# Banded attention with outputs by token, and products of masks in the openings of the stages

## The chip, the cores and the metric

One core of one Trainium2 chip runs the whole program in one launch. The metric is device time in microseconds. The kernel before took 4315.04 us (median of 3 runs, 4312.23 to 4320.44). TensorE multiplies matrices (PE in the profile, its weight loads PEld), VectorE is DVE, ScalarE is ACT, GpSimd is POOL, SyncE is SP and issues most transfers. TensorE's clock has two levels, 1.2 and 2.4 GHz; the profile shows the granted share, 0.50 or 1.00.

## The reference

Two blocks of a transformer run one after the other on 1024 latent tokens of width 1024, the first also on 256 context tokens. The first block has two hybrid layers. Each norms and modulates the tokens, projects them, and mixes them in three ways: latent attention (6 heads), banded attention (6 query heads on 2 key heads) and a short convolution; then come an output product and 16 experts of which each takes its best tokens. The second block has gated linear attention, differential attention and a large feed-forward part. The change's larger half is in the banded attention:

```python
s_loc = jnp.einsum('bqgrd,bkgd->bgrqk', q_b, k_b).astype(jnp.float32) * SWA_SCALE
s_loc = jnp.where(valid, s_loc, -jnp.inf)           # |query - key| <= 128
s_ctx = jnp.einsum('bqgrd,bcgd->bgrqc', q_b, k_ctx).astype(jnp.float32) * SWA_SCALE
p = sink_softmax(jnp.concatenate([s_ctx, s_loc], axis=-1), sink).astype(v.dtype)
return (jnp.einsum('bgrqc,bcgd->bqgrd', p[..., :n_ctx], v_ctx)
        + jnp.einsum('bgrqk,bkgd->bqgrd', p[..., n_ctx:], v_b))
```

A block of 128 queries sees the 256 context tokens and the local keys of its own, the previous and the next block. `sink_softmax` adds one learned score per head, the sink, which takes part in the sum and has no value. In the first layer the context tokens also attend to themselves, with the same sink.

## The kernel before

The program is a series of stages. A stage is one block of the five engines' instruction streams (`k.stage()`), with a barrier between two of them, so no work of one stage runs beside another's. Inside a stage the engines are ordered by semaphores alone, each stream in the order in which it is written. Most products are made in three parts: both operands are split into a high part that ScalarE rounds and a low part that VectorE or GpSimd subtracts, and TensorE adds high x high, high x low and low x high. In the opening of such a stage TensorE therefore waits for the first split tiles.

Stages of a hybrid layer, in order, with the function and the line of the first TensorE instruction: `project_in` (1618), `window_attention` (983), `latent_projections` (1176), `latent_attention` (1297), `mixed` through `residual` and `split_linear` (792), `route` (1909), `experts` (2283), `combine` (2463). The second block runs `project2` (through `scaled_linear`, 675), `linear_attention`, `differential_attention` (2987), `residual` again (792), `feed_up` (`scaled_linear`, 675), `feed_down` (3491) and `embed_and_finish` (3320).

`window_attention` works in units: a unit is one block of 128 queries and one head. Layer 0 has 2 context blocks and 8 latent ones, 60 units; layer 1 has 48. A unit has 2 key tiles of 128 (context block), 4 (first and last latent block) or 5. For unit u:

- TensorE, `scores(u)` (lines 983 to 986): queries against keys in two passes each, and a product of a mask for a tile that is partly hidden. Scores of two units fit in PSUM, so `scores(u)` waits for the exponentials of u-2.
- VectorE, `maxima(u)` (1099, 1100): maximum of each row, and the bias for the exponentials.
- ScalarE, `exps(u)` (1054): the exponentials; then at 1058 the exponential of the sink for this unit, as a 128 x 128 tile.
- TensorE, `turned(u)` (995): one transpose for each key tile. ScalarE copies the first four back (1071), VectorE the fifth (1126).
- TensorE, `products(u)`: the sink's tile times the identity (1005), then for each tile the values (64 columns, and 64 columns of ones) as stationary operand against the turned probabilities as moving one (1012). The output has features on partitions 0 to 63 and the sums on 64 to 127, by query in columns.
- VectorE, `outputs(u)`: reciprocal of the 64 x 128 sums (1107), and the product into the mixed tensor (1109).

TensorE's loop is `turned(u)`, `scores(u+2)`, `products(u)`. ScalarE's is the copy of u, then `exps(u+1)`. VectorE's is the fifth tile of u, `maxima(u+2)`, `outputs(u-1)`. Once a block, after its third head, ScalarE and VectorE split the queries of the block after next (1046, 1092). At the start VectorE builds the sinks' tile (1113, 1115) before the first maximum.

Of the kernel before, what the change touches and what calls it, by code (L numbers as in the profile page):

```python
# [13 lines left out]
ALU = mybir.AluOpType  # L14
# [3 lines left out]
P = 128  # L18
# [48 lines left out]
class Kernel:  # L67
# [59 lines left out]
    def part(self, off, *shape):  # L127

        return self.at(off, *shape, dt=F32R)

# [510 lines left out]
def scaled_linear(k, M, w_tile, scaled, wring, whi, evict, act_work=None, dve_work=None, sync_work=None, pe_work=None):  # L641
# [4 lines left out]
    with k.stage() as (block, sem):  # L646
# [16 lines left out]
        def _(pe):  # L663
            for n in range(M):
# [79 lines left out]
def split_linear(k, M, KT, chunks, w_tile, x, evac, engines, wring, make=None, before=None, beside=None, whi=None, wide=P):  # L744
# [9 lines left out]
    with k.stage() as (block, sem):  # L754
# [22 lines left out]
        def _(pe):  # L777
            if m:
                m.begin(pe)
# [142 lines left out]
def window_attention(k, l, with_ctx):  # L922
# [9 lines left out]
    NB, H = NLAT // P, 6  # L932
    o = XT0
# [4 lines left out]
    sinks, es = k.at(o, H, P), k.at(o + H * P, 2, P)  # L938
    o += (H + 2) * P
    pr = k.at(o, 2, 5 * P)  # L940
    o += 10 * P
    pt, rec = k.at(TAB0 + 1280, 2, 5, P), k.at(TAB0 + 1280 + 10 * P, 2, P)
    mx, nb = k.at(o, 64), k.at(o + 64, 64)
    assert o + 128 <= HT0
# [7 lines left out]
    half = lambda g: slice(64 * g, 64 * g + 64)  # L952

    with k.stage() as (block, sem):
        k_hi, k_lo, q_hi, q_lo, s_full, nb_set, p_set, sk_set, own = [sem() for _ in range(9)]
        t_full, pt_a, pt_b, pv_done, r_set, o_out, blank = [sem() for _ in range(7)]
# [4 lines left out]
        def _(pe):  # L961
            def scores(u):
# [70 lines left out]
        def _(act):  # L1033
# [14 lines left out]
            def exps(u):  # L1048
                h = units[u][2]
# [16 lines left out]
            for u in range(N):  # L1066
                act.wait_ge(t_full, count_t(u) + 1)
# [4 lines left out]
                if u + 1 < N:  # L1072
                    exps(u + 1)
                if u % H == 2 and 2 <= u // H + 1 < len(blocks):
                    queries(u // H + 1)

        @block.vector
        def _(dve):
# [23 lines left out]
            def outputs(u):  # L1102
                kind, b, h = units[u]
                t0 = tokens(kind, b)
                out = k.bank[6 + u % 2]
                dve.wait_ge(pv_done, u + 1)
                dve.reciprocal(rec[0:64, u % 2, :], out[64:P, 0:P]).then_inc(r_set, 1)
                dve.wait_ge(r_set, u + 1)
                dve.tensor_tensor(MIX[half(h % 2), 3 + h // 2, t0:t0 + P], out[0:64, 0:P], rec[0:64, u % 2, :], ALU.mult).then_inc(o_out, 1)
# [11 lines left out]
            for u in range(N):  # L1121
# [11 lines left out]
            outputs(N - 1)  # L1133
# [6 lines left out]
def latent_projections(k, l, with_ctx):  # L1140
# [14 lines left out]
    with k.stage() as (block, sem):  # L1155
# [11 lines left out]
        def _(pe):  # L1167
            for x, (kind, m, t0, n) in enumerate(items):
# [67 lines left out]
def latent_attention(k, l, with_ctx):  # L1236
# [47 lines left out]
    with k.stage() as (block, sem):  # L1284
# [4 lines left out]
        def _(pe):  # L1289
            def rough(p):  # L1290
# [212 lines left out]
def project_in(k, l, with_ctx):  # L1503
# [37 lines left out]
    with k.stage() as (block, sem):  # L1541
# [26 lines left out]
        def _(pe):  # L1568
            def sums(n):
# [281 lines left out]
def route(k, l, with_ctx):  # L1851
# [26 lines left out]
    with k.stage() as (block, sem):  # L1878
# [25 lines left out]
        def _(pe):  # L1904
            def raw(c):
# [238 lines left out]
def experts(k, l, with_ctx):  # L2144
# [37 lines left out]
    with k.stage() as (block, sem):  # L2182
# [85 lines left out]
        def _(pe):  # L2268
            def transposes(e, i, j, steady):
# [165 lines left out]
def combine(k, l, with_ctx):  # L2435
# [7 lines left out]
    with k.stage() as (block, sem):  # L2443
# [10 lines left out]
        def _(pe):  # L2454
            for i in range(len(tiles)):
# [478 lines left out]
def differential_attention(k):  # L2934
# [30 lines left out]
    with k.stage() as (block, sem):  # L2965
# [8 lines left out]
        def _(pe):  # L2974
# [716 lines left out]
```

## Time and profile before

| | |
|---|---|
| median of 3 runs | 4315.04 us |
| profiled execution | 4315.07 us, span 4313.3 us |
| TensorE busy | 3876.7 us, 90% |
| TensorE weight loads | 3083.9 us, 71% |
| VectorE, ScalarE, GpSimd busy | 2183.9, 1300.4 and 511.2 us (51%, 30%, 12%) |
| granted clock over the span | 0.946 |
| banded attention, first to last product | 301.8 to 466.8 us and 1741.3 to 1879.2 us |

The span begins with the program's first instruction on the core. TensorE's records overlap, since products are pipelined; the distance between two starts is what a product costs in a series, not its length. A wait is put down to whoever ended it. The clock share of a window is a mean: a window of 0.50 was wholly at the low level.

### The profile page before, as it was taken

How to read it: one execution, taken by the hardware profiler on the slowest of the kernel's cores; microseconds unless marked ns; L12 is line 12 of the kernel's file. 1: busy time of each engine (PE TensorE's matmuls, PEld its weight loads, DVE VectorE, ACT ScalarE, POOL GpSimd, SP SyncE). 2: the span in 40 equal slices, each digit the busy share in tenths (PEclk: the TensorE clock that was granted, in tenths of full speed). 3: DMA queues.
4: the chain of work that ended last, by engine and by line, in shares of the span. 5: the costliest groups of instructions: out<-in, count | busy, mean ns of one | idle time of the engine just before them, and what ended most of it. 6: DMA issues, size and time to landing. Idle time of an engine off the chain costs nothing. (4 is left out here: it accounts for less than half of the span.)

```text
span 4313.3 us, 51341 instructions
## 1 busy us (share of the span) xinstructions
PE 3876.7 (90%) x20508; PEld 3083.9 (71%) x20508; DVE 2183.9 (51%) x3383; ACT 1300.4 (30%) x2259; POOL 511.2 (12%) x601
## 2 busy tenths in 40 slices
PE   7989899887999889889985998799777899998997
PEld 5879665665777679866664998587555688887875
DVE  3479666333222256876534333583664465553344
ACT  3226533231111042553313333312453211112241
POOL 1010211103222110021012111100102100000011
PEclk9999899998999999989997999899888999999998
DMA  6100000448777431000025996212001211112111
GB/s 253 35 20 1 17 1 0 176 161 352 274 275 272 158 137 40 1 17 1 1 90 222 341 341 226 73 49 88 3 1 69 73 49 47 46 49 81 49 57 59
DMA packets 73877, 453.29 MB, mean 105 GB/s; under 512 B 8000, under 2 KB 12624, under 8 KB 57680
## 3 DMA queue, kind: packets, MB, share of 16 engines
q1 hardware_dynamic: 56960, 389.73, 24.0%
q0 software_dynamic: 13088, 47.19, 4.0%
q10 hardware_dynamic: 3632, 13.63, 0.8%
q8 instruction: 137, 2.24, 0.2%
q14 instruction: 60, 0.49, 0.0%
HBM read 394.95 MB, written 55.57 MB: 104 GB/s over the span
## 5 line engine op out<-in xcount | busy, mean ns | idle before, releaser
L2307 PEld LDWEIGHTS psum<-words,words 128*128 128x128 f32 x4096 | 513.9, 192 | 10.5 <-issue 9.2
L2307 PE MATMUL psum<-words,words 128*128 128x160 f32 (+1 forms) x4096 | 515.2, 288 | 1.5 <-DVE words L392 1.5
L675 PE MATMUL psum<-words,words 128*128 128x512 f32 x1104 | 442.3, 401 | 31.0 <-DVE words L715 26.6
L677 PE MATMUL psum<-words,words 128*128 128x512 f32 x1104 | 438.0, 397 | 0.0
L676 PE MATMUL psum<-words,words 128*128 128x512 f32 x1104 | 437.9, 397 | 0.0
L1618 PE MATMUL psum<-words,words 128*128 128x428 f32 (+1 forms) x720 | 253.3, 352 | 31.7 <-DVE words L1711 31.7
L675 PEld LDWEIGHTS psum<-words,words 128*128 128x128 f32 x1104 | 209.3, 190 | 83.7 <-DVE words L715 28.1
L1327 PE MATMUL psum<-words 128*128 128x512 f32 (+1 forms) x504 | 252.3, 582 | 0.0
L1619 PE MATMUL psum<-words,words 128*128 128x428 f32 (+1 forms) x720 | 250.0, 347 | 0.0
L1620 PE MATMUL psum<-words,words 128*128 128x428 f32 (+1 forms) x720 | 249.4, 346 | 0.0
L694 ACT ACTIVATE words<-words 128x1024 fp32r<-128x1024 f32 x69 | 73.1, 1060 | 582.3 <-DMA words<-in_w_up 382.0
L677 PEld LDWEIGHTS psum<-words,words 128*128 128x128 f32 x1104 | 209.2, 189 | 51.1
L676 PEld LDWEIGHTS psum<-words,words 128*128 128x128 f32 x1104 | 208.8, 189 | 51.0 <-issue 1.0
L1371 ACT ACTIVATE words<-psum 128x512 f32<-128x512 f32 (+1 forms) x252 | 147.7, 586 | 283.3 <-PE psum L1319 283.3
L1397 DVE TENSOR_REDUCE words<-psum 128x1 f32<-128x512 f32 (+1 forms) x300 | 163.3, 587 | 120.3 <-PE psum L1297 119.5
L792 PE MATMUL psum<-words,words 128*128 128x512 f32 (+1 forms) x448 | 173.8, 388 | 33.3 <-DVE words L515 33.1
L1317 PE MATMUL psum<-words,words 97*128 97x512 f32 (+1 forms) x252 | 195.3, 775 | 9.2 <-ACT words L1358 9.2
L591 POOL TENSOR_TENSOR words<-words 128x512 f32<-128x512 f32 (+1 forms) x56 | 76.2, 1393 | 1020.7 <-ACT words L584 1020.7
L2404 DVE TENSOR_TENSOR words<-words,psum 128x160 f32<-128x160 f32 x64 | 20.6, 322 | 316.3 <-ACT words L2367 316.3
L794 PE MATMUL psum<-words,words 128*128 128x512 f32 (+1 forms) x448 | 172.1, 384 | 0.0
L793 PE MATMUL psum<-words,words 128*128 128x512 f32 (+1 forms) x448 | 171.5, 383 | 0.0
L1618 PEld LDWEIGHTS psum<-words,words 128*128 128x128 f32 x720 | 138.1, 192 | 37.0 <-DVE words L1711 32.1
(438 smaller groups left out, 7853.2 us busy)
## 6 DMA issues: line engine op xcount, KB each, us to landing
words<-in_w_gate SPq DMA_DIRECT2D x32, 2048.0 KB, 8.2
words<-in_w_up SPq DMA_DIRECT2D x32, 2048.0 KB, 12.7
words<-in_w_down SPq DMA_DIRECT2D x32, 2048.0 KB, 13.1
words<-in_ada_w SPq DMA_DIRECT2D x24, 2048.0 KB, 14.7
words<-in_w_in SPq DMA_DIRECT2D x55, 512.0 KB, 3.4
words<-in_w_up SPq DMA_DIRECT2D x44, 512.0 KB, 3.4
words<-in_w_down SPq DMA_DIRECT2D x44, 256.0 KB, 2.6
words<-in_x SPq DMA_DIRECT2D x2, 5120.0 KB, 22.0
```

The source lines that it names most:

```text
L675: pe.matmul(out, hi[:, j, w], S.parts[0](kt, t0, nt), start=(kt == 0), stop=False)
L676: pe.matmul(out, hi[:, j, w], S.parts[1](kt, t0, nt), start=False, stop=False)
L677: mm = pe.matmul(out, lo[:, j, w], S.parts[0](kt, t0, nt), start=False, stop=(kt == KD - 1))
L792: pe.matmul(out, hi[:, j, w], x[0](kt, t0, n), start=(kt == 0), stop=False)
L793: pe.matmul(out, hi[:, j, w], x[1](kt, t0, n), start=False, stop=False)
L794: mm = pe.matmul(out, lo[:, j, w], x[0](kt, t0, n), start=False, stop=(kt == KT - 1))
L1317: pe.matmul(to, k_hi[0:ROW + 1, h % 2, key], q_hi[0:ROW + 1, h % 2, t0:t0 + n], start=True, stop=False)
L1327: pe.matmul(k.bank[O_BANK[u % 2]][:, 0:n], V[:, 6 * t + h, :], pt[:, x % R, 0:n], start=(t == 0), stop=(t == keys - 1)).then_inc(d_done, 1)
L1618: pe.matmul(out, whi[:, j, w], xhi[:, kt, c0:c0 + nc], start=(kt == 0), stop=False)
L1619: pe.matmul(out, whi[:, j, w], xlo[:, kt, c0:c0 + nc], start=False, stop=False)
L1620: mm = pe.matmul(out, wlo[:, j, w], xhi[:, kt, c0:c0 + nc], start=False, stop=(kt == KD - 1))
L2307: mm = pe.matmul(k.bank[m % 2][:, u * W:(u + 1) * W], ring[:, side[j], w0:w0 + P], xgT[:, j, kt, 0:W], start=(kt == 0), stop=(kt == KD - 1))
```

## The change

Two things are changed.

First, `keep_busy` is called at the head of TensorE's stream in twelve functions, 22 stages in all. It makes n products of 128 x 128 by 128 x 384, both operands from the constant masks (bf16), into PSUM bank 7. Nobody reads them, and they wait for nothing but the barrier. The numbers are 16 (`scaled_linear`), 20 (`split_linear`), 9 or 23 (`window_attention` of layers 0 and 1), 7 (`latent_projections`), 5 (`latent_attention`), 22 (`project_in`), 6 (`route`), 70 or 16 (`experts` of layers 0 and 1), 9 (`combine`), 5 (`differential_attention`), 16 (`embed_and_finish`), 16 (`feed_down`).

Second, in `window_attention` the value product changes sides: the turned probabilities are stationary and the values moving, 64 features and one column of ones. The output is by token: queries on partitions, and the six heads of a block side by side in one PSUM bank, 72 columns apart. The sink's tile and its product are gone. Once a block VectorE subtracts the sinks from the six biases (`arguments`), ScalarE takes six exponentials a row (`sinks`), VectorE adds them to the six sums, takes six reciprocals and norms all heads in one product (`outputs`); TensorE turns the result back with three transposes (`back`), and VectorE copies it into the mixed tensor (`place`). ScalarE's order in a unit is changed too.

```diff
+    def keep_busy(self, pe, n, bank=7):
+        for _ in range(n):
+            pe.matmul(self.bank[bank][:, 0:3 * P], self.bmask[:, 2 * P:3 * P], self.bmask[:, 0:3 * P],
+                      start=True, stop=True, skip_group_check=True)
...
             def products(u):
                 kind, b, h = units[u]
-                if u >= 2:
-                    pe.wait_ge(o_out, u - 1)
-                pe.wait_ge(sk_set, u + 1)
-                out = k.bank[6 + u % 2][:, 0:P]
-                pe.matmul(out, es[:, u % 2, :], k.ident[:, :], start=True, stop=False)
+                n = u // H
+                if h == 0 and n >= 2:
+                    pe.wait_ge(placed, n - 1)
...
-                    mm = pe.matmul(out, SV[:, 2 * tile + h % 2, :], pt[:, u % 2, t, :], start=False, stop=(t == tiles(u) - 1))
+                    mm = pe.matmul(k.bank[6 + n % 2][:, h * WIDE:h * WIDE + 65], pt[:, u % 2, t, :], SV[:, 2 * tile + h % 2, 0:65],
+                                   start=(t == 0), stop=(t == tiles(u) - 1), skip_group_check=True)
...
+            def back(n):
+                pe.wait_ge(o_out, n + 1)
+                for f in range(3):
+                    mm = pe.transpose(k.bank[6 + n % 2][:, f * P:(f + 1) * P], flat(heads[:, n % 2, 2 * f:2 * f + 2, :]), k.ident[:, :])
+                mm.then_inc(backed, 1)
...
                 products(u)
+                if u > H and u % H == 2:
+                    back(u // H - 1)
+            back(N // H - 1)
...
-                if u >= 2:
-                    act.wait_ge(pv_done, u - 1)
-                act.activation(es[:, u % 2, :], sinks[:, h, :], ACT.Exp, bias=nb[:, u:u + 1]).then_inc(sk_set, 1)
+            def sinks(n):
+                act.wait_ge(args_set, n + 1)
+                act.activation(es[:, n % 2, 0:H], es[:, n % 2, 0:H], ACT.Exp).then_inc(sk_set, 1)
...
             for u in range(N):
+                if u + 1 < N:
+                    exps(u + 1)
                 act.wait_ge(t_full, count_t(u) + 1)
...
                 act.activation(pt[:, u % 2, 0:n, :], k.bank[4][:, 0:n * P].rearrange("p (a b) -> p a b", b=P), ACT.Copy).then_inc(pt_a, 1)
-                if u + 1 < N:
-                    exps(u + 1)
                 if u % H == 2 and 2 <= u // H + 1 < len(blocks):
                     queries(u // H + 1)
+                if u % H == H - 1:
+                    sinks(u // H)
...
+            def arguments(n):
+                dve.wait_ge(nb_set, H * (n + 1))
+                dve.tensor_tensor(es[:, n % 2, 0:H], nb[:, H * n:H * (n + 1)], sink, ALU.subtract).then_inc(args_set, 1)
+
+            def outputs(n):
+                e = es[:, n % 2, 0:H]
+                per_head = e.rearrange("p (h a) -> p h a", a=1)
+                dve.wait_ge(sk_set, n + 1)
+                dve.wait_ge(pv_done, H * (n + 1))
+                if n >= 2:
+                    dve.wait_ge(backed, n - 1)
+                link(dve.tensor_tensor(per_head, sums(n)[:, :, 64:65], per_head, ALU.add))
+                link(dve.reciprocal(e, e))
+                dve.tensor_tensor(heads[:, n % 2], sums(n)[:, :, 0:64], per_head.to_broadcast([P, H, 64]), ALU.mult).then_inc(o_out, 1)
+
+            def place(n):
+                t0 = tokens(*blocks[n])
+                dve.wait_ge(backed, n + 1)
+                dve.tensor_copy(MIX[:, 3:6, t0:t0 + P], k.bank[6 + n % 2][:, 0:3 * P].rearrange("p (f c) -> p f c", c=P)).then_inc(placed, 1)
...
-            link(dve.memset(sinks[:, :, 0:64], -1e30))
-            for h in range(H):
-                link(dve.tensor_scalar(sinks[:, h, 64:P], k.ones[:, 0:64], sink[:, h:h + 1], -1.0, ALU.mult, ALU.mult))
...
                 if u + 2 < N:
                     maxima(u + 2)
-                if u:
-                    outputs(u - 1)
+                    if (u + 2) % H == H - 1:
+                        arguments((u + 2) // H)
+                if u > H:
+                    if u % H == 1:
+                        outputs(u // H - 1)
+                    if u % H == 4:
+                        place(u // H - 1)
```

## Rows read from the trace of the kernel before

**Rows 1.** Windows: stretch, length, busy us of PE, PEld, DVE, ACT, POOL, clock, DMA.
```profile
347.00:447.00 100.00, 97.94 (x869) 95.68 (x868) 91.32 (x184) 60.92 (x117) 0.00 (x0) 1.00 0.01 1
```

**Rows 2.** Timeline of TensorE's weight loads: start, length, engine, line, operation, tiles, shapes, count.
```profile
403.49 0.58 PEld L995 LDWEIGHTS psum<-ident,words 128*128 128x128 f32 x5
404.03 0.19 PEld L983 LDWEIGHTS psum<-words,words 128*128 128x128 f32 x1
404.92 0.31 PEld L1005 LDWEIGHTS psum<-ident,words 128*128 128x128 f32 x2
405.15 1.20 PEld L1012 LDWEIGHTS psum<-words 128*128 128x128 f32 x10
406.27 0.58 PEld L995 LDWEIGHTS psum<-ident,words 128*128 128x128 f32 x5
```

**Rows 3.** Windows, sum line of the eight dense openings at the low clock.
```profile
sum 40.57, PE 39.04 PEld 33.71 DVE 25.76 ACT 27.02 POOL 0.00; mean PE 4.88 PEld 4.21 DVE 3.22 ACT 3.38 POOL 0.00
```

**Rows 4.** Windows, sum line of the three openings of the split product.
```profile
sum 15.62, PE 15.61 PEld 13.12 DVE 15.62 ACT 15.62 POOL 15.62; mean PE 5.20 PEld 4.38 DVE 5.21 ACT 5.21 POOL 5.21
```

**Rows 5.** Windows, sum line of the five short openings.
```profile
sum 21.33, PE 21.32 PEld 10.31 DVE 9.02 ACT 11.21 POOL 1.96; mean PE 4.26 PEld 2.06 DVE 1.80 ACT 2.24 POOL 0.39
```

**Rows 6.** Groups by line: records | busy us, mean ns | idle before.
```profile
L1012 PE MATMUL psum<-words 128*128 128x128 f32 x960 | 126.7, 277 | 0.9 <-ACT words L1071 0.9
```

**Rows 7.** Timeline of TensorE in the first stage, eight records of 2 columns.
```profile
34.40 1.05 PE L279 MATMUL psum<-add,words 128*128 128x2 f32 x8
```

**Rows 8.** Timeline of TensorE, last mask of that unit's scores.
```profile
404.92 0.23 PE L986 MATMUL psum<-bmask 128*128 128x128 bf16 x1
```

**Rows 9.** Timeline of VectorE in the same unit.
```profile
405.19 0.82 DVE L1099 TENSOR_REDUCE words<-psum 128x1 f32<-128x640 f32 x1
406.05 0.21 DVE L1100 TENSOR_SCALAR words<-words,negsink 128x1 f32<-128x1 f32 x1
406.29 0.96 DVE L1107 RECIPROCAL words<-psum 64x128 f32<-64x128 f32 x1
407.29 0.28 DVE L1109 TENSOR_TENSOR words<-psum,words 64x128 f32<-64x128 f32 x1
```

**Rows 10.** Timeline of ScalarE in the same unit.
```profile
404.23 0.60 ACT L1071 ACTIVATE words<-psum 128x512 f32<-128x512 f32 x1 [1.21 <-PE psum L995]
404.73 0.79 ACT L1054 ACTIVATE words<-psum,words 128x640 f32<-128x640 f32 x1
```

**Rows 11.** Groups by line and shape, a copy of 384 columns from PSUM.
```profile
L392 DVE COPY words<-psum 128x384 f32<-128x384 f32 x10 | 5.6, 558 | 5.6 <-PE psum L1181 5.5
```

**Rows 12.** Timeline of VectorE in a context unit.
```profile
315.60 0.42 DVE L1099 TENSOR_REDUCE words<-psum 128x1 f32<-128x256 f32 x1
```

**Rows 13.** Timeline of ScalarE in a context unit.
```profile
314.92 0.38 ACT L1071 ACTIVATE words<-psum 128x256 f32<-128x256 f32 x1 [1.22 <-PE psum L995]
315.20 0.47 ACT L1054 ACTIVATE words<-psum,words 128x256 f32<-128x256 f32 x1
```

**Rows 14.** Timeline of VectorE, opening of banded attention in layer 1.
```profile
1741.79 1.71 DVE L1115 TENSOR_SCALAR words<-ones,negsink 128x64 f32<-128x64 f32 x6
```

**Rows 15.** Timeline of TensorE, first stage of layer 0, clock rising.
```profile
61.54 0.56 PE L1619 MATMUL psum<-words,words 128*128 128x428 f32 x1
61.90 0.56 PE L1620 MATMUL psum<-words,words 128*128 128x428 f32 x1
...
62.95 0.35 PE L1618 MATMUL psum<-words,words 128*128 128x428 f32 x1
63.15 0.35 PE L1619 MATMUL psum<-words,words 128*128 128x428 f32 x1
```

**Rows 16.** Timeline of VectorE, opening of the split product after differential attention.
```profile
3290.30 13.65 DVE L515 TENSOR_TENSOR words<-words,words 128x512 fp32r<-128x512 f32 x8
```

**Rows 17.** Timeline of VectorE, opening of latent attention in layer 0.
```profile
518.58 6.35 DVE L1397 TENSOR_REDUCE words<-psum 128x1 f32<-128x512 f32 x12
```

**Rows 18.** Timeline of TensorE while the experts' results are combined in layer 0.
```profile
1500.69 1.09 PE L2463 MATMUL psum<-ident,words 128*128 128x128 f32 x8 [0.25 <-DMA words<-moe]
```

More of the change, by code:

```diff
@@ L663, in _ @@
         def _(pe):
+            k.keep_busy(pe, 16)
             for n in range(M):
@@ L777, in _ @@
         def _(pe):
+            k.keep_busy(pe, 20)
             if m:
@@ L931, in window_attention @@
     prev, nxt, idb = (k.bmask[:, n * P:(n + 1) * P] for n in range(3))
-    NB, H = NLAT // P, 6
+    NB, H, WIDE = NLAT // P, 6, 72
     o = XT0
@@ L937, in window_attention @@
     o += 12 * P
-    sinks, es = k.at(o, H, P), k.at(o + H * P, 2, P)
-    o += (H + 2) * P
+    heads = k.at(o, 2, H, 64)
+    o += 6 * P
     pr = k.at(o, 2, 5 * P)
     o += 10 * P
-    pt, rec = k.at(TAB0 + 1280, 2, 5, P), k.at(TAB0 + 1280 + 10 * P, 2, P)
-    mx, nb = k.at(o, 64), k.at(o + 64, 64)
-    assert o + 128 <= HT0
+    pt = k.at(TAB0 + 1280, 2, 5, P)
+    mx, nb, es = k.at(o, 64), k.at(o + 64, 64), k.at(o + 128, 2, 8)
+    assert o + 144 <= HT0
     blocks = ([(0, c) for c in range(CT)] if with_ctx else []) + [(1, b) for b in range(NB)]
@@ L952, in window_attention @@
     half = lambda g: slice(64 * g, 64 * g + 64)
+    sums = lambda n: k.bank[6 + n % 2][:, 0:H * WIDE].rearrange("p (h c) -> p h c", c=WIDE)
     with k.stage() as (block, sem):
         k_hi, k_lo, q_hi, q_lo, s_full, nb_set, p_set, sk_set, own = [sem() for _ in range(9)]
-        t_full, pt_a, pt_b, pv_done, r_set, o_out, blank = [sem() for _ in range(7)]
+        t_full, pt_a, pt_b, pv_done, args_set, o_out, blank, backed, placed = [sem() for _ in range(9)]
         pieces = ([(0, NCTX), (NCTX, NLAT)] if with_ctx else [(0, NT)])
@@ L961, in _ @@
         def _(pe):
+            k.keep_busy(pe, 9 if with_ctx else 23)
             def scores(u):
@@ L1048, in exps @@
             def exps(u):
-                h = units[u][2]
                 act.wait_ge(nb_set, u + 1)
@@ L1100, in maxima @@
                 dve.tensor_scalar(nb[:, u:u + 1], mx[:, u:u + 1], -SWA_SCALE, sink[:, h:h + 1], ALU.mult, ALU.min).then_inc(nb_set, 1)
[L1102 to L1109, printed above, removed]
+            def arguments(n):
[15 more added lines that the diff above has]
+                dve.tensor_copy(MIX[:, 3:6, t0:t0 + P], k.bank[6 + n % 2][:, 0:3 * P].rearrange("p (f c) -> p f c", c=P)).then_inc(placed, 1)
             queries(0)
             keys_of(0)
-            link(dve.memset(sinks[:, :, 0:64], -1e30))
-            for h in range(H):
-                link(dve.tensor_scalar(sinks[:, h, 64:P], k.ones[:, 0:64], sink[:, h:h + 1], -1.0, ALU.mult, ALU.mult))
             maxima(0)
@@ L1128, in _ @@
                     maxima(u + 2)
-                if u:
-                    outputs(u - 1)
+                    if (u + 2) % H == H - 1:
[5 more added lines that the diff above has]
+                        place(u // H - 1)
                 if u % H == 2 and 2 <= u // H + 1 < len(blocks):
                     queries(u // H + 1)
-            outputs(N - 1)
+            outputs(N // H - 1)
+            place(N // H - 1)
 KT0, V0 = PR0 + 6 * NT, PR0 + 12 * NT
@@ L1167, in _ @@
         def _(pe):
+            k.keep_busy(pe, 7)
             for x, (kind, m, t0, n) in enumerate(items):
@@ L1289, in _ @@
         def _(pe):
+            k.keep_busy(pe, 5)
             def rough(p):
@@ L1568, in _ @@
         def _(pe):
+            k.keep_busy(pe, 22)
             def sums(n):
@@ L1904, in _ @@
         def _(pe):
+            k.keep_busy(pe, 6)
             def raw(c):
@@ L2268, in _ @@
         def _(pe):
+            k.keep_busy(pe, 70 if with_ctx else 16)
             def transposes(e, i, j, steady):
@@ L2454, in _ @@
         def _(pe):
+            k.keep_busy(pe, 9)
             for i in range(len(tiles)):
@@ L2974, in _ @@
         def _(pe):
+            k.keep_busy(pe, 5)
             def scores(n):
@@ L3297, in _ @@
         def _(pe):
+            k.keep_busy(pe, 16)
             def shares(n):
@@ L3480, in _ @@
         def _(pe):
+            k.keep_busy(pe, 16)
             for s in range(S):
```

## The prediction

> **What bounds the kernel now.** The kernel is a series of 25 stages with a barrier between two of them, so what one stage loses or gains passes to the end unchanged; the span is read stage by stage. I read the windows first. Inside banded attention of the first layer TensorE is busy for 97.94 of 100 us at clock 1.00, VectorE for 91.32 and ScalarE for 60.92 [rows 1]. One (block, head) unit there with five key tiles has 25 TensorE records (5 transposes, 6 score products, 2 masks, 2 of the sink product at line 1005, 10 of line 1012), so 869 records are 34.8 units, 2.87 us each. The timeline of weight loads shows the inside of one [rows 2]: transposes 403.49 to 404.03 (0.54), scores to 404.92 (0.89), sink product to 405.15 (0.23), value products to 406.27 (1.12), sum 2.78, with no hole; the other 0.09 of the mean is where the next queries are split. So TensorE's count of passes sets the pace, and VectorE is close behind. Then I read the openings of the stages: TensorE has been idle, and its first work runs at clock 0.50 although it is busy. In the eight dense openings (both projections, both expert stages, `project2`, feed up, feed down, embed) that is 40.57 us [rows 3], in the three of the split product at lines 792 to 794 15.62 [rows 4], in five short ones 21.33 [rows 5]. These are the two places that the change touches. The profiled execution took 4315.07 us (span 4313.3), the median is 4315.04: I subtract from 4315.
>
> **Banded attention, TensorE.** Removed for each of 108 units: the sink product, 0.23. The value products keep their number: two records a tile, 960 for 480 tiles [rows 6]. They change sides: probabilities become the stationary operand (still 128 columns), values the moving one, 65 columns instead of 128. No row has 65 columns. Bounds: eight records with 2 moving columns take 1.05 us, with the length of one record (0.23, rows 8) off (1.05 - 0.23)/7 = 0.117 a pass [rows 7, 8], and with 128 columns a pass takes 1.12/10 = 0.112 [rows 2]. The ends agree to 0.005, so the stationary load sets the pass, and I take 0.112: no change.
> The Trainium skill, "TensorE: Matmul & The Clock Gate", LDWEIGHTS, puts a load at its columns over 1.2 GHz, 107 ns for 128, whatever moves; by it the value products stay as they are, and the rows agree. The same page, Back-to-back issue gap, has a product cost its moving columns over 2.4 GHz plus 2.5 ns; by that one they would get cheaper (first rival).
> Added: three transposes for a block of six units, 3 x 0.112 = 0.34, or 0.06 a unit. Its wait is for the normed outputs, which VectorE starts a whole unit earlier; behind it stand only the next unit's transposes. TensorE's own work is then 2.78 - 0.23 = 2.55.
>
> **The chain through the four engines.** ScalarE now does the exponentials of unit u+1 before it copies the turned tiles of unit u. From the start T of a unit's transposes: the scores of the unit after next end at T+0.54+0.89+0.23 (the last mask's own length, [rows 8]) = 1.66, the maximum starts at 1.70, takes 0.82 with 0.04 behind it, the bias 0.21 [rows 9]: 2.77. The exponentials follow; ScalarE's next instruction starts some 0.68 later (0.79 less an overlap of 0.1, as 404.23 to 404.73 is for a copy of 0.60), and the copy takes 0.60 [rows 10]: 4.08. That copy belongs to the next unit, whose value products TensorE could begin at P + 1.43, P the period. So P = 2.55 + (4.08 - 1.43 - P), which gives P = 2.60. The order of ScalarE costs 0.05. If the copy hides wholly, P is 2.55; if latencies are 0.17 worse twice over, it is 2.78. I take 2.60, as all terms but the order are measured. With the transposes 2.66 a unit, against 2.87: 0.21 x 72 units = 15 us. The 0.09 at the queries goes, because VectorE loses the reciprocal of 0.96 and the product of 0.28 in each unit [rows 9] and gets per block an addition, a reciprocal of six columns (each no more than about the 0.21 of a bias), a product and a copy of 384 columns from PSUM, 0.56 each [rows 11]: 1.24 a unit becomes 1.6/6 = 0.27. ScalarE loses one activation a unit.
> Context units (12, two tiles): VectorE sets them, 0.42 + 0.21 + 0.96 + 0.28 and gaps, 2.0. After, TensorE has (2+2+4) x 0.112 = 0.9 and the same chain runs 0.45 + 0.3 + 0.42 + 0.04 + 0.21 + 0.03 + 0.36 + 0.38 = 2.2 [rows 12, 13], so P = (2.2 + 0.45)/2 = 1.33; with 0.06, 0.6 saved each, 7 us; the first run at the low clock, so 6. Units of four tiles (24) stand between: 0.2 each, 5 us.
> Opening: in the second layer the first maximum waits behind the six operations at line 1115, 1.71 us [rows 14], which go; in the first layer ScalarE is later anyway. I take 1.3. End: after the last product there were 0.96 + 0.28; now three small operations, 0.34 of transposes and a copy, 2.0: 0.8 lost, twice. Sum: 15 + 5 + 6 + 1.3 - 1.6 = 26. Bounds 13 (P of 2.78) and 30 (P of 2.55).
>
> **Masks in 22 openings.** A pass of 428 columns takes 0.36 at the low clock and 0.20 at the high one [rows 15], so a stretch at the low clock gives back 0.45 of itself. By columns I estimate a mask of 384 at 0.36 x 384/428 = 0.32 cold, 0.18 warm. They lie in a wait for operands that other engines make, so they cost nothing as long as they end before those; only the 70 of the first expert stage, 22 us at the low clock, are longer than the wait, and they should be warm after some microseconds.
> Dense openings: 40.57 x 0.45 = 18.3 [rows 3]. Split products: TensorE is then fed by VectorE, 13.65 us for 8 tiles while GpSimd makes the other 8 [rows 16], so 0.85 a tile against the 0.6 it needs warm; of 6.1 us about 1.7 come back, 0.28 of 15.62 = 4.4. Short openings: the masks (7, 7, 6, 6, 5) only bring the rise forward by their own 31 x 0.32 = 9.9, x 0.45 = 4.5. Latent attention opens with twelve maxima on VectorE back to back, 6.35 us [rows 17]: nothing. Combining waits for its own loads [rows 18]: nothing. Banded attention's are counted above. Sum 27. But between the last mask and the first operand TensorE is idle again, 1 to 2 us, and the low clock can be back by then; the trace of before cannot show it. Bounds 0 and 27, I take two thirds: 18.
>
> **Rivals.** (1) The narrower moving operand does count: a pass of 65 columns at 0.112 x 65/128 = 0.057. Then TensorE's own work is 2.00, P = (2.65 + 2.00)/2 = 2.33, 0.27 x 72 = 19 more, with the others about 26: 4245. For it: it streams half as much; against it: [rows 7]. (2) The masks bring nothing, since the clock falls again in the pause or the operands limit all openings: 26 alone, 4289. For it: TensorE falls to 0.50 after each pause between stages; against: in the dense openings little is left between masks and first product. (3) Slower: the stationary operand is now a tile that ScalarE has just written, and 960 loads of it are no longer pulled ahead of the product before. If a pass then took the length of a load record, 0.19, it would cost 0.08 x 960 = 77, less 44: 33 slower, 4348. It decides from 0.112 + 44/960 = 0.158 a pass. Against it: the transposes, too, take a tile that ScalarE has just written, at 0.54/5 [rows 2].
>
> **How the numbers follow.** Forecast: 26 + 18 = 44, 4271 us. Chances: forecast 0.66, rival (2) 0.14, (1) 0.07, (3) 0.06, both parts small 0.07. The forecast's own range is 4259 (29 + 27) to 4296 (13 + 6); with rival (2) inside and half of (1) reached, 4254 to 4296. What can be told from no change here is 0.2%, 9 us. Faster 0.66 + 0.14 + 0.07 + 0.03 = 0.90, same 0.03, slower 0.07.
>
> **What would show it.** Right: five-tile units every 2.6 us; value products still 0.11 apart; a period without the bump at the queries; clock 1.00 at the first products of the dense openings, and these at 0.20 instead of 0.36. Wrong: a ScalarE copy ending later than 1.5 us into a unit; the clock at 0.50 at the first product; passes over 0.15 apart; the first product of a stage later than the operands it waits for.

## The result: faster by 0.7%, but not by the sum predicted

The kernel after takes 4289.37 us (median of 7 runs, 4283.15 to 4300.96), the kernel before 4318.57 (7 runs, 4312.23 to 4323.39). The ratio is 0.9932, 95% interval 0.992 to 0.9945: 29 us less, where 44 were forecast. The time lies inside the range (4254 to 4296), at the figure that the prediction gave to its rival (2), 4289, the masks bringing nothing. That is a coincidence: the masks brought 21 us instead of 18, and attention some 6 to 7 instead of 26, under the 13 that the prediction took as attention's lower bound. The sum stayed in the range because its lower end also took only 6 us for the masks, so that the time lies inside it is in part luck.

### The profile after

The profiled execution took 4297.97 us, span 4296.1, against a span of 4313.3 before: 17.2 less. First the page's line of busy time by engine, then two of its groups by line (records | busy us, mean ns | idle before):

```profile
PE 3948.0 (92%) x20691; PEld 3101.0 (72%) x20691; DVE 2079.7 (48%) x3243; ACT 1274.4 (30%) x2169; POOL 511.4 (12%) x601
L1020 PE MATMUL psum<-words 128*128 128x65 f32 x960 | 139.3, 294 | 8.5 <-ACT words L1093 6.0
L134 PE MATMUL psum<-bmask 128*128 128x384 bf16 x345 | 86.9, 425 | 85.4 <-PEq L144 85.4
```

The 960 value products kept their number and changed their width. With about half the moving columns their busy time went up, 139.3 us against 126.7 [rows 6]; the next views show why.

Windows of the kernel after: context units of layer 0, the stretch that answers to [rows 1], and layer 1's opening (columns as in [rows 1]).

```profile
307.80:332.00 24.20, 23.68 (x99) 20.64 (x100) 10.19 (x31) 11.15 (x27) 0.00 (x0) 0.50 0.00 1
335.00:435.00 100.00, 99.03 (x874) 95.14 (x872) 63.68 (x153) 56.29 (x96) 0.00 (x0) 1.00 0.01 1
1738.30:1758.80 20.50, 19.70 (x95) 19.23 (x96) 4.92 (x12) 7.26 (x13) 0.00 (x0) 0.50 0.00 1
```

And the context units of the kernel before, a stretch that the prediction gives no window of:

```profile
308.40:333.30 24.90, 18.65 (x127) 16.50 (x128) 21.59 (x48) 14.04 (x39) 0.00 (x0) 0.93 0.00 1
```

In the middle of the stage VectorE fell from 91.32 to 63.68 of 100 us, and TensorE's clock is 1.00, as forecast. In the context units TensorE is busy for 23.68 of 24.20 us and yet its granted clock is 0.50, the lower level of 1.2 GHz. Before, it was busy for 18.65 of 24.90 us there and had 0.93. Layer 1 shows the same low stretch.

The timeline of weight loads over one five-tile unit, which answers to [rows 2], and behind it that of the products of a context unit (start, length):

```profile
397.99 0.59 PEld L1005 LDWEIGHTS psum<-ident,words 128*128 128x128 f32 x5
398.55 0.19 PEld L993 LDWEIGHTS psum<-words,words 128*128 128x128 f32 x1
...
399.43 1.21 PEld L1020 LDWEIGHTS psum<-words 128*128 128x128 f32 x10
400.50 0.59 PEld L1005 LDWEIGHTS psum<-ident,words 128*128 128x128 f32 x5
...
319.08 1.11 PE L1020 MATMUL psum<-words 128*128 128x65 f32 x4
319.99 0.63 PE L1005 MATMUL psum<-ident,words 128*128 128x128 f32 x2
...
321.10 1.11 PE L1020 MATMUL psum<-words 128*128 128x65 f32 x4
```

The five-tile unit takes 400.50 - 397.99 = 2.51 us, without the sink product, and its ten value products 1.07, so 0.107 a pass. A context unit takes 321.10 - 319.08 = 2.02, with no hole in TensorE: it was 2.0 before, bound by VectorE.

The opening of the first projection in layer 0, TensorE's timeline, first the answer to [rows 15]:

```profile
49.29 5.12 PE L134 MATMUL psum<-bmask 128*128 128x384 bf16 x22 [8.79 <-PEq L144]
56.80 0.46 PE L1658 MATMUL psum<-words,words 128*128 128x428 f32 x1 [2.39 <-DVE words L1751]
57.10 0.35 PE L1659 MATMUL psum<-words,words 128*128 128x428 f32 x1
57.29 0.36 PE L1660 MATMUL psum<-words,words 128*128 128x428 f32 x1
57.49 0.35 PE L1658 MATMUL psum<-words,words 128*128 128x428 f32 x1
```

Passes 0.20 apart from the second product on, where before they stood 0.36 apart until 62.25. The pause of 2.39 us between the last mask and the first product did not bring the low clock back here.

Here is where the 17 us of the profiled pair went, by the length of each stage from barrier to barrier (after less before). It is one profiled execution each. In most stages the profiles of the twelve kernels agree within a microsecond or two where nothing was changed. But routing in layer 0 lies anywhere between 93.9 and 100.8 us, differential attention between 183.4 and 190.5, and `project2`, with the same masks, between 312.7 and 317.3. So the row of the short openings can't be read to better than some 7 us, and that of the dense stages to better than some 4:

```
                               after - before   masks only (e1) - before
banded attention (2)               -7.0              +0.1
dense stages (8)                  -11.1             -14.2
split products (3)                 -2.1              -1.1
short openings (5)                 -4.1              -6.9
latent attention (2)               +3.0              +2.0
combining the experts (2)          +3.8              +2.6
all others                         +0.2              +1.7
sum                               -17.3             -15.8
```

### The profile page after: what moved, and what is told of

The parts are those of the page before. It is cut to its first block and busy times, and to the rows that moved or that the text cites. A ratio compares the mean times of both kernels' runs of the same rounds, so it can differ in the third digit from the quotient of the medians.

```text
span 4296.1 us, 51403 instructions
## 1 busy us (share of the span) xinstructions
PE 3948.0 (92%) x20691; PEld 3101.0 (72%) x20691; DVE 2079.7 (48%) x3243; ACT 1274.4 (30%) x2169; POOL 511.4 (12%) x601
## 5 line engine op out<-in xcount | busy, mean ns | idle before, releaser
L2349 PEld LDWEIGHTS psum<-words,words 128*128 128x128 f32 x4096 | 510.9, 191 | 10.3 <-issue 9.1
L682 PE MATMUL psum<-words,words 128*128 128x512 f32 x1104 | 440.7, 399 | 14.2 <-DVE words L722 9.8
L682 PEld LDWEIGHTS psum<-words,words 128*128 128x128 f32 x1104 | 208.7, 189 | 66.9 <-DVE words L722 11.4
L684 PEld LDWEIGHTS psum<-words,words 128*128 128x128 f32 x1104 | 208.5, 189 | 50.7
L683 PEld LDWEIGHTS psum<-words,words 128*128 128x128 f32 x1104 | 207.9, 188 | 50.8 <-issue 1.0
L134 PE MATMUL psum<-bmask 128*128 128x384 bf16 x345 | 86.9, 425 | 85.4 <-PEq L144 85.4
```

The costliest lines, as they stand in the source:

```text
L682: pe.matmul(out, hi[:, j, w], S.parts[0](kt, t0, nt), start=(kt == 0), stop=False)
L683: pe.matmul(out, hi[:, j, w], S.parts[1](kt, t0, nt), start=False, stop=False)
L684: mm = pe.matmul(out, lo[:, j, w], S.parts[0](kt, t0, nt), start=False, stop=(kt == KD - 1))
L2349: mm = pe.matmul(k.bank[m % 2][:, u * W:(u + 1) * W], ring[:, side[j], w0:w0 + P], xgT[:, j, kt, 0:W], start=(kt == 0), stop=(kt == KD - 1))
```

## The experiments

Ratios are to the kernel before, timed beside it on the same chip, with 95% intervals; a gain in us is the ratio times 4319. "Low clock" is the time at 0.50 after the first product of the stage, read in each profile.

**e1, masks alone.** The kernel before with the masks of all twelve functions, attention unchanged.

```
+    def keep_busy(self, pe, n, bank=7): ...
         def _(pe):
+            k.keep_busy(pe, 16)
...                        (eleven more functions, each with its own number)
```

> The kernel before with the masks at the head of the 22 openings, banded attention untouched. Theory A (the masks give back part of the low clock in dense openings, and lose some where their instruction fetch meets the first load; the rest of the change gives only some 7 us as profiled): 4299 to 4310, ratio 0.9955 to 0.9985, banded attention stages of 170.0 and 147 us as before. Rival B (the masks give two thirds of 27 us, as predicted): ratio 0.9958 or under, 4300 or under. Rival C (the masks give all 29 us of the change): ratio 0.993.

Measured: 0.9951 (0.9937 to 0.9964), 4299.18 us: 21 us, as rival B has it and more than theory A. The masks are worth a little more than the 18 taken, and the prediction's rival (2) falls.

**e2, attention alone.** The kernel after without its masks.

```
         def _(pe):
-            k.keep_busy(pe, 16)
...
```

> The changed kernel without any mask products. Theory A (the new banded attention runs its five-tile units in 2.67 instead of 2.90 us, but its stages stay long at the low clock because of what TensorE does in them, masks or not): stage of layer 0 163 to 166 us against 170.0, low clock for over 20 us of it; ratio 0.995 to 0.998. Rival B (the low clock in the stage came from where the masks ended): low clock for 10 to 17 us at the opening, stages of about 155 and 138 us, ratio 0.994 or under.

Measured: 0.9987 (0.9978 to 0.9996), 4317.59 us: some 6 us (2 to 10) instead of 26. So the two parts add up, 21 + 6 = 27 against 29, and the missing gain is attention's. Its window of the context units:

```profile
308.40:332.20 23.80, 23.25 (x97) 20.21 (x98) 10.05 (x31) 10.73 (x27) 0.00 (x0) 0.50 0.00 1
```

The low clock there is not a matter of the masks in front: without them it is 37.4 us in layer 0 and 30.0 in layer 1. The stages (163.7 and 147.0 us) and the clock are as theory A has them; the ratio is above its 0.995 to 0.998.

**e3, 128 moving columns.** The kernel after; a value product streams all 128 columns of its tile instead of 65, with the same count of products. The further columns of the result are not read.

```
-  mm = pe.matmul(k.bank[6 + n % 2][:, h * WIDE:h * WIDE + 65], pt[:, u % 2, t, :], SV[:, 2 * tile + h % 2, 0:65],
+  mm = pe.matmul(k.bank[6 + n % 2][:, h * WIDE:h * WIDE + P], pt[:, u % 2, t, :], SV[:, 2 * tile + h % 2, :],
```

> The changed kernel with 128 moving columns in the value product instead of 65 (each head's surplus columns are overwritten by the next head's first product). Theory A (a pass costs 0.112 us at either width, and with 65 columns TensorE is seen as less busy, so the clock stays low): five-tile units stay at 2.5 to 2.7 us, low clock in the stages falls from 34 and 25 us to under 15 each, stages of about 155 and 139 us, ratio to before 0.988 to 0.990. Rival B (width has nothing to do with the clock): same as the changed kernel, 0.993. Rival C (128 columns cost more a pass): five-tile units over 2.8 us, slower than the changed kernel by 10 us.

Measured: 0.9915 (0.9901 to 0.9928), 4283.68 us. This overlaps with the kernel after (0.992 to 0.9945), so the times alone would not settle it; the stages do: 157.1 and 140.9 us instead of 163.8 and 146.7, with 6.9 and 8.4 us of low clock instead of 34.1 and 25.4. The clock did what theory A says; the stages are 2 us longer than it says, and the ratio misses its 0.990. Its windows, and TensorE's timeline in the context units:

```profile
308.00:311.80 3.80, 3.53 (x13) 2.94 (x14) 1.25 (x5) 1.84 (x5) 0.00 (x0) 0.50 0.00 0
311.80:328.00 16.20, 13.70 (x100) 11.77 (x100) 9.76 (x30) 10.26 (x26) 0.00 (x0) 1.00 0.01 2
```

```profile
318.65 0.71 PE L1020 MATMUL psum<-words 128*128 128x128 f32 x4 [0.23 <-ACT words L1093]
319.20 0.38 PE L1005 MATMUL psum<-ident,words 128*128 128x128 f32 x2
...
320.06 0.71 PE L1020 MATMUL psum<-words 128*128 128x128 f32 x4 [0.23 <-ACT words L1093]
```

A context unit is now 320.06 - 318.65 = 1.41 us and TensorE waits in each for ScalarE's copy: the chain that the prediction priced at 1.33. Streaming twice the columns made it shorter by 0.6. A pass at 1.00 takes 0.112 against 0.107 with 65 columns. That would be 0.05 for a five-tile unit; here it is 0.02 (2.69 against 2.67), since half of the units wait for ScalarE's copy at either width.

**e4, ScalarE's old order.** The kernel after with the exponentials of unit u+1 again behind the copy of unit u.

```
             for u in range(N):
-                if u + 1 < N:
-                    exps(u + 1)
                 act.wait_ge(t_full, count_t(u) + 1)
...
                 act.activation(pt[:, u % 2, 0:n, :], k.bank[4]... .then_inc(pt_a, 1)
+                if u + 1 < N:
+                    exps(u + 1)
```

> The changed kernel with ScalarE's old order (copy of unit u, then the exponentials of u+1). Theory A of the prediction (the new order costs 0.05 us a unit, since the copy waits for the exponentials): five-tile units 2.55 to 2.6 us, ratio to before 0.992, 4 us better than the changed kernel. Rival B (with the old order the exponentials come late for the next transposes and scores, the new order is needed): units of 2.8 us or more, 10 us worse, ratio 0.9955.

Measured: 0.9902 (0.9886 to 0.9917), 4280.52 us, clear of the kernel after and better than theory A's 0.992. The timeline of ScalarE in a five-tile unit, of the kernel after and then of e4, and three windows of e4: the middle of the stage, its context units, and layer 1 from the rise of its clock on:

```profile
398.05 0.80 ACT L1072 ACTIVATE words<-psum,words 128x640 f32<-128x640 f32 x1 [1.23 <-DVE words L1122]
398.75 0.60 ACT L1093 ACTIVATE words<-psum 128x512 f32<-128x512 f32 x1
400.81 0.80 ACT L1072 ACTIVATE words<-psum,words 128x640 f32<-128x640 f32 x1 [1.46 <-DVE words L1122]
```

```profile
398.67 0.60 ACT L1091 ACTIVATE words<-psum 128x512 f32<-128x512 f32 x1 [1.23 <-PE psum L1005]
399.16 0.79 ACT L1072 ACTIVATE words<-psum,words 128x640 f32<-128x640 f32 x1
```

```profile
335.00:435.00 100.00, 99.57 (x906) 97.45 (x906) 66.51 (x162) 57.55 (x99) 0.00 (x0) 1.00 0.01 1
310.00:332.00 22.00, 21.58 (x92) 18.83 (x92) 9.39 (x28) 8.75 (x24) 0.00 (x0) 0.50 0.00 1
1741.90:1758.80 16.90, 16.62 (x149) 16.04 (x149) 8.90 (x23) 9.26 (x17) 0.00 (x0) 1.00 0.00 1
```

In the kernel after ScalarE waits for the bias of the next unit (DVE, L1122), and the copy that TensorE needs stands behind it; in e4 it waits only for the transposes. Periods in a block: 2.51, 2.70, 2.51, 2.76, 2.51, 3.03 after, mean 2.67; 2.51, 2.51, 2.51, 2.52, 2.51, 2.85 in e4, mean 2.57. The order costs 0.10 a unit, twice the 0.05 of the prediction: 0.10 x 72 = 7 us. The second window has TensorE low in layer 0 as in the kernel after (28.0 us in all). In layer 1, the third window, it rose after 9.5 us instead of 25.4, and the first block of four-tile units took 15.2 us instead of 21.6. So 65 columns do not hold the clock down in every case, and why it rose there is open: the order of ScalarE alone need not be the reason, since layer 0 has it too.

**e5, both.** e3 and e4 together.

> 128 moving columns and ScalarE's old order together. Theory A (two separate effects: width keeps the clock up in units of two and four tiles, the order saves 0.1 us a five-tile unit): five-tile units 2.6 us in the mean, context units 1.4 to 1.5, low clock under 15 us in each stage, stages of about 152 and 135 us, ratio to before 0.988 to 0.990. Rival B (with the full width TensorE is the bound at 2.56 + 0.06 anyway and the order brings nothing more): stages as with 128 columns alone, 157 and 141 us, ratio 0.9915.

Measured: 0.9901 (0.9883 to 0.9918), 4276.64 us; stages 153.9 and 137.5, low clock 7.6 and 8.4, as theory A has it but for 2 us in each stage. In its middle:

```profile
335.00:435.00 100.00, 99.79 (x890) 97.70 (x890) 65.48 (x158) 56.40 (x97) 0.00 (x0) 1.00 0.01 1
```

TensorE has no hole, and the mean unit is 2.62: e4's 2.57 with ten passes 0.005 longer. Layer 0 gains 9.9 us on the kernel after (6.7 in e3, 6.1 in e4), layer 1 9.2 (5.8 and 11.3). By time e5 is not to be told from e4.

**e6 and e9, fillers beside 65 columns.** The kernel after with one (e6) or three (e9) mask products of 384 columns behind the values of each context unit, two behind those of each four-tile unit, into a bank part that nobody reads. TensorE was busy nearly all the time already, so this asks whether what it streams matters.

```
                 mm.then_inc(pv_done, 1)
+                if tiles(u) < 5:
+                    for _ in range(2 if kind else 1):            # e9: 3
+                        pe.matmul(k.bank[5][:, P:4 * P], k.bmask[:, 2 * P:3 * P], k.bmask[:, 0:3 * P], start=True, stop=True, skip_group_check=True)
```

> The changed kernel (65 columns, its own order) with one mask product behind the values of each context unit and two behind those of each four-tile unit, which nobody reads. Theory A (what keeps the clock low is how little TensorE streams in these units): the clock rises within the first units although there is more work, context units go from 2.01 to about 1.5 us, low clock in the stages from 34 and 25 us to under 15; ratio 0.991. Rival B (the width of the value product itself matters, for instance by its output rows): clock stays low, context units 2.3 us and four-tile units of layer 1 about 4.1 us, ratio 0.995.

> As e6, but three mask products behind the values of each context unit instead of one (the value product still has 65 columns). Theory A (more streaming beside the 65-column products brings the clock up): the clock rises within the first three or four context units, which then take about 1.9 us (2 x 0.17 more than the 1.5 of e6); low clock in the stage of layer 0 under 15 us. Rival B (one mask or three, the rise in e6 at the tenth unit came from the longer units behind): low clock for 25 us and more, context units 3.0 us. No faster than e6 either way: ratio 0.991 to 0.994.

Measured: e6 0.9923 (0.9909 to 0.9936), e9 0.9948 (0.993 to 0.9966). Windows of the context units, e6, then e9:

```profile
307.20:326.70 19.50, 19.13 (x76) 15.84 (x76) 6.10 (x20) 7.68 (x19) 0.00 (x0) 0.50 0.00 1
```

```profile
311.80:331.00 19.20, 17.07 (x121) 13.46 (x119) 9.39 (x29) 9.94 (x25) 0.00 (x0) 1.00 0.00 1
```

With one filler the clock stayed at 0.50 until the ninth of the twelve context units (2.33 us a unit, then down to 1.51); with three it rose at the third (then 1.84 a unit). In layer 1 both had none at 0.50 after the first product, and the stage fell to 140.9 and 141.0 from 146.7. So with the value products left at 65 columns the clock rises earlier the more is streamed beside them: low clock in layer 0 is about 34, 26 and 11 us with none, one and three fillers, and 25 and 0 in layer 1 with none and two. In layer 0 e6 does not reach theory A's 15 us and e9 does. There the fillers cost what the clock gives (165.7 and 164.8 against 163.8). The ratio of e9 is above the 0.991 to 0.994 expected of it, though its two stages together are no longer than e6's; the intervals overlap.

**e7, 128 columns without masks.** e3 without any mask in an opening.

> The changed kernel with 128 moving columns and without the masks of the openings. Theory A (masks and width are independent): ratio 0.9987 x 0.9915/0.9932 = 0.997 or lower, stages of banded attention about 158 and 140 us, low clock in the first under 17 us. Rival B (the clock rises in the context units only if the masks have raised it before): stage of layer 0 at 163 us with over 30 us of low clock, ratio 0.9987.

Measured: 0.9961 (0.9947 to 0.9974), 4304.07 us: 17 us from attention alone, against 6 with 65 columns (e2), the intervals apart; theory A holds. The stages are 157.9 and 141.0, as in e3 with masks.

```profile
307.20:313.30 6.10, 5.96 (x23) 5.07 (x24) 2.03 (x7) 2.58 (x6) 0.00 (x0) 0.50 0.00 0
313.30:327.00 13.70, 11.42 (x83) 9.70 (x83) 8.82 (x26) 8.70 (x23) 0.00 (x0) 1.00 0.01 2
```

Between e2 and e7 only the width of the value products differs, and with it the low clock goes from 37.4 and 30.0 us to 12.8 and 8.2. The masks in front of attention matter little to it.

**e8, masks in six functions.** The kernel before with masks only where dense and split-product stages open (`scaled_linear`, `split_linear`, `project_in`, `experts`, `embed_and_finish`, `feed_down`).

> The kernel before with masks only where TensorE is busy throughout its opening (the three linear helpers, projection, experts, feed down, embed: 11 stages), none in banded and latent attention, latent projections, route, combine and differential attention. Theory A (the gain of the masks comes from these 11 openings, 23 us by the prediction's terms less what is lost): ratio 0.995, as with all 22. Rival B (the short openings carry a third of it): ratio 0.9967.

Measured: 0.9963 (0.995 to 0.9977), 4306.84 us: 16 us, against 21 for all twelve. The other six would bring some 5, near rival B; but the interval holds the ratio of theory A (0.995) as well as that of rival B (0.9967) and overlaps with e1's, so the run doesn't decide between them.

**e10, masks in the gap.** e5, with more masks between the scores of the second unit and the first transposes, where TensorE waits for the first exponentials.

```
             scores(1)
+            k.keep_busy(pe, 26 if with_ctx else 8)
             for u in range(N):
```

> e5 (128 columns and the old order) with 26 more masks in layer 0 and 8 in layer 1 between the first scores and the first transposes of banded attention, where TensorE waits for ScalarE. Theory A (the clock falls in that wait and its first units run low): low clock of the two stages falls from 7.6 and 8.4 us to under 5, stages 1 to 3 us shorter (151 to 153 and 135 to 136), ratio 0.989 to 0.990. Rival B (the masks end too late or the clock falls anyway): stages as long or 1 to 2 us longer.

Measured: 0.9893 (0.9874 to 0.9911), 4268.94 us: the fastest of all, 46 us under the kernel before, and clear of the kernel after. Stages 152.4 and 135.1, as theory A has it; after the first product of either stage there is no low clock left. Its timeline of TensorE and the windows of both openings:

```profile
303.07 4.40 PE L134 MATMUL psum<-bmask 128*128 128x384 bf16 x26
309.19 0.44 PE L1005 MATMUL psum<-ident,words 128*128 128x128 f32 x2 [1.72 <-ACT words L1073]
```

```profile
302.40:326.30 23.90, 19.70 (x134) 15.47 (x135) 14.99 (x40) 16.84 (x36) 0.00 (x0) 1.00 0.00 1
1726.30:1745.00 18.70, 18.14 (x155) 17.23 (x155) 9.45 (x22) 9.92 (x17) 0.00 (x0) 1.00 0.00 1
```

From e5 to e10 the two stages lose 1.5 + 2.4 = 3.9 us, which is the step between the ratios (0.0008 of 4319 is 3.5 us); by the intervals e10 is not to be told from e5.

## Why the prediction was right, and where it was wrong

**Value products by pass: right.** 0.107 with 65 columns and 0.112 with 128, against 0.112 taken. Rivals (1), at 0.057, and (3), at 0.19, fall. The Trainium skill, "TensorE: Matmul & The Clock Gate", LDWEIGHTS, which puts the load of 128 columns at 107 ns, has the trace on its side at the high clock. The formula from its Back-to-back issue gap, on which rival (1) leaned, would give 65 columns 0.03 (an estimate from its figures). The page gives it for a product by itself, and says of a stream of loads and products that both set the spacing; so it is no price for these passes, each of which brings its own stationary tile, and the trace has 0.107.

**Five-tile units: right in sum.** 2.67 us against 2.66, down from 2.89: 0.22 x 72 = 16 against 15. Inside it two errors cancel: TensorE's own work is 2.51 instead of 2.55, and ScalarE's order costs 0.10 instead of 0.05. The bump at the queries went, as forecast. What is left of it is something else: every sixth unit is at 3.03, and at 2.85 in e4, 0.34 over the others, because the three transposes of `back` stand in it. These are weight loads of e4: the value products of a unit, `back` (0.33 to the next start), and the next unit's transposes:

```profile
399.35 1.21 PEld L1020 LDWEIGHTS psum<-words 128*128 128x128 f32 x10
400.43 0.37 PEld L1028 LDWEIGHTS psum<-ident,words 128*128 128x128 f32 x3
400.76 0.58 PEld L1005 LDWEIGHTS psum<-ident,words 128*128 128x128 f32 x5
```

That is the prediction's 3 x 0.112, or 0.06 a unit.

**Context and four-tile units: this step failed.** It priced the context units at 1.33 each, "the first run at the low clock", and the four-tile units at 0.2 less each, all for the clock of before, which rose soon. It asked of the narrower moving operand only whether a pass gets shorter, and never whether TensorE would still come to its full clock. With 65 columns it did not for 34 and 25 us. The two stages of attention, cut at the first value product of each block (less before, us):

```
                                   forecast   after    e2      e3 (128 columns)
five-tile units (72)                 -15      -15.7   -15.8   -14.0
context units (12)                    -6       +0.4    +0.3    -6.0
four-tile units (24)                  -5       +7.1    +7.1    -0.2
openings                              -1.3     -1.5    -0.9    -1.5
after the last value product          +1.6     +2.6    +2.6    +2.2
sum                                  -26       -7.0    -6.8   -19.5
```

- Context units: 2.02 each in the kernel after instead of 1.33, so nothing gained. With 128 columns the 6 us of the forecast are there.
- Four-tile units: the first block of layer 1 alone is 6.4 us longer than before (3.55 a unit and more, 2.28 in e3), at the low clock. But at 128 columns, with the clock up, the 24 units together still gain only 0.2 us. So of the 12 us by which this term missed, 7 are the clock and 5 are the "0.2 each" itself, which the prediction put down without a working. Why so little comes there was not traced.
- The ends: 1.3 lost in each layer instead of 0.8; 0.4 of it is the low clock of the last transposes (2.68 us from the last value product to the end of the stage, 2.32 in e3's layer 0, 1.36 before).

e3, e5, e7 show the cause from one side (same count of passes, wider products, clock up, 1.41 a context unit), e6 and e9 from the other (65 columns kept, something else streamed, clock up earlier). Two things are not explained: that the clock rose in e4's layer 1 with 65 columns, and that in the kernel after it is 1.00 in all five-tile units with the same 65 columns. The tail's end, from VectorE, answers to the 2.0 of the prediction:

```profile
458.70 0.17 DVE L1136 TENSOR_TENSOR words<-psum,words 128x6 f32<-128x6 f32 x1 [5.47 <-issue]
458.90 0.19 DVE L1137 RECIPROCAL words<-words 128x6 f32<-128x6 f32 x1
459.12 0.56 DVE L1138 TENSOR_TENSOR words<-psum,words 128x384 f32<-128x384 f32 x1
460.67 0.56 DVE L1143 COPY words<-psum 128x384 f32<-128x384 f32 x1 [0.99 <-PE psum L1028]
```

From 458.70 to 461.23 it is 2.5, with the transposes at low clock between (0.90 in the records, where the three take 0.50 at 1.00). VectorE's batch with its copy is 1.48 a block, against 1.6 priced.

**Masks: mechanism right, size off by little.** 21 us (e1) against 18 taken; bounds 0 to 27. The discount of a third for the pause behind the masks was more than needed: after 2.39 us of idling the first products still ran at 0.20. In the eight dense openings the low clock after the first product fell from 40.6 us before to 6.8 in e1, which by the 0.45 of the prediction is 15.2 us, and their stages lost 14.2 (18.3 undiscounted), 3.9 of it in `project2`, which is less sure. All of the 6.8 is in two of them, feed up and embed, which have the longest pauses of the eight between the last mask and the first product, 3.1 and 3.2 us; the other six, with 0.6 to 1.6 us, have none. In the three split products the low clock fell from 15.7 to 3.4 us and the stages lost only 1.1 (4.4 priced): the clock rose, but the pace did not. In the first 14 us behind its first product TensorE starts 60, 51 and 51 products in e1 and 60, 50 and 49 before, as the engines that split the operands set it [rows 16], more than the prediction allowed for. The short openings lost 6.9 (4.5 priced), of which 4.3 are differential attention, within what that stage varies by itself. The prediction says of the masks of banded attention that they are counted above; no term above counts them, and e1's attention stages, 170.1 and 147.5, are as before.

**Latent attention and combining: "nothing" stands.** Both lost in e1 and in the kernel after, but not through the masks. Latent attention of layer 0 took 265.5 us before, 268.4 in the kernel after, 267.9 in e1 and 268.5 in e9, but 265.2 to 265.8 in five other kernels with the same masks, and 267.3 in e7 without any. Combining in layer 0 took 33.8 before and 35.6 and 36.2 in those two, but 33.5 to 33.7 in e3, e4, e6, e9 and e10, and 35.2 in e7. Combining opens with masks that end before the operands arrive:

```profile
1481.11 3.04 PE L134 MATMUL psum<-bmask 128*128 128x384 bf16 x9 [9.21 <-PEq L144]
1486.27 3.03 PE L2506 MATMUL psum<-ident,words 128*128 128x128 f32 x13 [2.12 <-DMA words<-moe]
```

The masks are not in the way: TensorE waits 2.12 us for a load. That load was late. Take the records of the transfers in the three openings that wait for their own load (latent projections of layer 0, combining of both layers), in all twelve kernels. Where no fetch of instructions (16 KB, queue q8) falls into the first 2.6 us behind the issue of the first load, that load lands after 2.5 to 3.4 us; where one does, after 3.8 to 5.8, without exception. In the kernel after all three have one (3.84, 5.16 and 5.01 us); before none. e2 and e7, without masks, each have one in one opening; e6, e9 and e10, with all masks, and e8, with those of six functions, have none. So it is not the masks' work that decides; it may be where the code of a stage falls in the stream, but this is a correlation without a run that moves the code alone. Latent attention's 3 us were not traced to a cause.

## What to carry to other kernels

- A cheaper form of a product that keeps its passes can cost the clock: read the granted clock of the stage, not only the length of a pass, and look at what the stretch streams. Where it matters, widen the moving operand to what costs no pass (here 65 to 128 columns: at most 0.05 for a five-tile unit, against 0.6 for a context unit), and try both.
- Products of masks in openings where TensorE waits for operands are worth having (21 us of 4319 here), and where a second pause follows, a second lot of them may be worth a try (e10: 3.9 us by the stages, not clear by the time).
- In an order written out by hand, put the instruction that feeds the bounding engine first; the exponentials ahead of the copy saved nothing and cost 7 us.

## What the runs showed of the hardware that was not expected

- TensorE busy for 23.68 of 24.20 us stays at 0.50 with value products of 65 columns, and is granted 0.93 with 18.65 of 24.90 us at 128 columns (the kernel before). Busy time does not tell the clock.
- The kernels with 65 columns and at most one filler a context unit (after, e2, e4, e6) had 26 to 37 us of low clock in layer 0; the six with 128 and none in the gap (before, e1, e3, e5, e7, e8) 7 to 13. Layer 1 varies more: 25.4, 30.0, 9.5 and 0.0 (e6, with two fillers a four-tile unit there) against 3.4 to 8.8.
- A fetch of instructions of 16 KB beside the first load of a stage goes with a delay of 1 to 2.5 us of that load, in 36 openings of twelve kernels without exception. Stages whose code did not change vary with it by as much as a small change gives, so the sum over stages of one profile is to be read with care.
